# Encoder trunk in fp32r: scores of three neighbourhood groups as 128-row products of stacked keys and queries

## The chip, the cores and the metric

One core of one Trainium2 chip runs the whole kernel in one launch. The metric is the device time of one execution in microseconds (us), the median over the timed runs. The engines are named as the profile names them: PE is TensorE's matmul, PEld its weight load, DVE VectorE, ACT ScalarE, POOL GpSimd, SP SyncE, which issues nearly all DMAs.

## The reference, cut to what matters

Two layers run on x, 1024 tokens by 1024 features, in fp32. Each layer takes h = RMSNorm(x), projects it to the queries, keys and values of two kinds of heads and to a gate, attends, multiplies by silu(gate), projects back and adds to x. A final RMSNorm follows.

```python
# differential heads: 4 heads, two 64-wide halves each
s = einsum('bqhcd,bkhcd->bhcqk', qi, k) * scale - slope * |i - j|
p = softmax(s); a = p[:, :, 0] - lam * p[:, :, 1]; o = a @ v
# neighbourhood heads: 8 heads of width 64, a grid of 16 rows x 64 columns
s = einsum('bnqhd,brnkhd->bhnqrk', qr, kb) * scale   # 8 grid rows, 16 columns around each query
s = where(col_valid, s + bias, -inf); p = softmax(s); o = p @ v
```

The change concerns only the products of queries and keys of the neighbourhood heads.

## The kernel before, in words

**Arithmetic.** Every fp32 operand of a product is split in two fp32r parts, hi (a rounded copy that ACT writes) and lo (the rest, a subtraction on DVE or POOL). A product of two such operands is three matmuls: hi times hi, hi times lo and lo times hi; lo times lo is left out. `three` (L1134) does this for the projections.

**Groups and steps.** A layer has eight groups (`Group`, L192): four of one differential head each, then four of two neighbourhood heads each. A group has eight query tiles of 128 tokens, one for each step t. While a group attends, PE also runs the projections in pieces (`group_piece`, 24 matmuls of 512 columns each, for half of the tokens): pieces 0 and 1 of a group are its own gate, 2 to 7 the values, keys and queries of the next group, two pieces each. Piece t runs in step t, piece 0 of the next group in step 8, split in three parts that stand between the attention work. The last neighbourhood group projects no next one (`project=False`); output rows fill its steps. `from_second` (L543) and `steps` (L530) walk the steps in the same order on each engine; the order within a step is written out by hand in PE's `step` (L1319), DVE's `step` (L1734), ACT's `attend` (L1005) and POOL's `attend` (L774).

**Scores.** `score` (L1158) computes the scores of both heads of a tile (m = 0 and 1). Head m has its 64 features in partitions 64m to 64m+63 of `q_hi`, `q_lo`, `k_hi` and `k_lo`, so each matmul contracts over 64 rows of the array; the inner loop goes over m, so two products stand next to each other that use different halves of the rows. A neighbourhood tile in positions 0 to 3 (image tiles 0, 1, 6, 7; "edge") has 512 keys, one in positions 4 to 7 (tiles 2 to 5; "inner") has 576, of which 64 are computed by separate matmuls, ahead for m = 0 and behind for m = 1 (`tail`, L1179). An edge tile takes 6 matmuls, an inner tile 12. PE runs `score` of tile t+1 in the middle of step t, between the two transposes of tile t-1's probabilities, and `score` of the next group's tile 0 in step 7, of its tile 1 in step 8.

**The other engines in a neighbourhood step.** DVE adds the bias and takes the row maxima (`shifted`, L1632); ACT takes the exponentials (`exponentials`, L960); POOL divides by the sums (`weigh_rows`, L740); PE transposes the result (`turn_p`, L1216, L1231); ACT writes the hi part (`p_part`, L951, L940), DVE the lo part (L1659); every second step PE multiplies by the values (`weigh_pair`, L1268, L1282 and L1283), ACT and DVE take the product out (`output_half`, L975; `output_pair`, L1701).

**Queries and keys of the next group.** DVE writes key pieces 4 and 5 to `k_next` and query pieces 6 and 7, one after the other, to `q_next` (`piece_part`, L1603). ACT copies them to `k_hi` (L936, in step 6, after PE has read the keys for the last time) and `q_hi` (L930, steps 6 and 8). DVE makes `k_lo` (L1630) at the start of step 7, POOL makes `q_lo` (`q_lo_part`, L709). POOL also makes the lo parts of the weights (`w_lo_part`, L693, 128 columns by 8), in step 6 those of the next group's gate, as soon as ACT has made the hi part (L898). `load_chunk` (L599) on SP loads the next weights when that lo part is done.

## Time and profile before

| | us |
|---|---|
| median of 3 runs | 1426.14 (1425.80 to 1426.84) |
| the profiled execution | 1425.85 |
| its span, first to last instruction | 1424.0 |
| PE busy, of the span | 1410.6 (99%) |
| POOL, DVE, ACT busy | 651.9, 879.0, 692.9 |
| mean granted TensorE clock | 0.998 of full |

The profiled execution took 1425.85 us as a run, 1.85 us more than the span of its records. A busy PE is not the same as a PE at its peak: matmuls are pipelined, and a record lasts from the first column in to the last result out, so neighbouring records overlap. The distance from start to start is what a matmul costs the stream.

### The profile page before, as it was taken

To read this page: it belongs to the slowest core of one execution; us is meant where nothing else is said; L and a number is where in the kernel's file an instruction comes from. 1 tells how busy PE (TensorE), PEld (TensorE's weight loads), DVE (VectorE), ACT (ScalarE), POOL (GpSimd) and SP (SyncE) were. 2 spreads that over 40 slices of the span, in tenths; PEclk is the share of its full clock that TensorE was granted. 3 is DMA by queue.
4 is the path that set the end of the run, shared out by engine and by line. 5 is a ranking of instruction groups with operands and counts; after the bars stand their busy time and mean duration, and the time that the engine had idled before them with its cause. 6 is when DMAs were issued, how large, how long until landed. Compare 5 with 4: busy or idle time off the path is not lost.

```text
span 1424.0 us, 23782 instructions
## 1 busy us (share of the span) xinstructions
PE 1410.6 (99%) x8148; PEld 1155.3 (81%) x8148; DVE 879.0 (62%) x1815; ACT 692.9 (49%) x1376; POOL 651.9 (46%) x490
## 2 busy tenths in 40 slices
PE   9999999999999999999999999999999999999997
PEld 7788887888888888788887887888888888887887
DVE  7767677767655565653337776767766555556434
ACT  6445555455444444652525555546454444457331
POOL 3223222234576667543643231323247666667243
PEclk9999999999999999999999999999999999999999
DMA  5710101121021112301210100100212121213113
GB/s 185 155 30 23 52 22 37 37 63 38 24 70 34 57 39 56 148 30 45 74 45 31 38 23 29 44 30 22 66 36 64 38 63 37 63 38 126 46 59 118
DMA packets 41850, 79.57 MB, mean 56 GB/s; under 512 B 19120, under 2 KB 21424, under 8 KB 41776
## 3 DMA queue, kind: packets, MB, share of 16 engines
q1 hardware_dynamic: 41632, 78.60, 17.6%
q8 instruction: 44, 0.72, 0.2%
q14 instruction: 30, 0.25, 0.1%
q10 hardware_dynamic: 144, 0.01, 0.0%
HBM read 66.57 MB, written 15.96 MB: 58 GB/s over the span
## 4 chain that ended last, share of the span: by engine, by line
PE 96%; DVE 1%; ACT 1%; issue 1%; DMA 1%; SPq 0%; POOLq 0%; POOL 0%; DVEq 0%; ACTq 0%
PE proj L1136 19%; PE proj L1138 19%; PE proj L1137 18%; PE scores L1172 12%; PE turn L1231 6%; PE mix L1282 3%; PE mix L1283 3%; PE scores L1231 2%; PE mix L1249 2%; PE mix L1248 2%; PE mix L1247 2%; PE scores L1136 1%; PE scores L1137 1%; PE scores L1138 1%; DMA xt<-x_t 1%
## 5 line engine op out<-in xcount | busy, mean ns | idle before, releaser
L1136 PE MATMUL proj<-h_hi,w_hi 128*128 128x512 f32 (+1 forms) x1184 | 487.3, 412 | 1.2 <-DVE h_lo L1534 1.1
L1138 PE MATMUL proj<-h_hi,w_lo 128*128 128x512 f32 (+1 forms) x1184 | 461.5, 390 | 0.0
L1137 PE MATMUL proj<-h_lo,w_hi 128*128 128x512 f32 (+1 forms) x1184 | 458.5, 387 | 0.0
L696 POOL TENSOR_TENSOR w_lo<-w_raw,w_hi 128x1024 fp32r<-128x1024 f32 x62 | 152.7, 2463 | 308.8 <-ACT w_hi L898 308.8
L1659 DVE TENSOR_TENSOR pt_lo<-turn,pt_hi 128x512 fp32r<-128x512 f32 (+1 forms) x208 | 139.1, 669 | 204.8 <-ACT pt_hi L940 203.5
L1138 PEld LDWEIGHTS proj<-h_hi,w_lo 128*128 128x128 f32 x1184 | 222.4, 188 | 49.2
L1136 PEld LDWEIGHTS proj<-h_hi,w_hi 128*128 128x128 f32 x1184 | 223.2, 188 | 41.8 <-issue 5.5
L1137 PEld LDWEIGHTS proj<-h_lo,w_hi 128*128 128x128 f32 x1184 | 224.0, 189 | 34.2
L940 ACT ACTIVATE pt_hi<-turn 128x512 fp32r<-128x512 f32 (+1 forms) x208 | 120.4, 579 | 202.4 <-PE turn L1231 201.1
L747 POOL TENSOR_SCALAR prob<-prob,rrec 128x512 f32<-128x512 f32 (+1 forms) x96 | 156.9, 1647 | 113.2 <-DVE rrec L1684 112.8
L1651 DVE CUSTOM_DVE_ANT_0 prob<-scores,inner 128x1024 f32<-128x1024 f32 (+1 forms) x192 | 203.5, 1060 | 3.6 <-PE scores L1172 3.2
L965 ACT ACTIVATE prob<-prob,nm,escale_now 128x1024 f32<-128x1024 f32 x128 | 158.7, 1239 | 57.5 <-DVE nm L1655 57.1
L1231 PE MATMUL turn<-ident,prob 128*128 128x128 f32 x768 | 118.6, 277 | 0.0
L965 ACT ACTIVATE prob<-prob,nm 128x576 f32<-128x576 f32 (+1 forms) x128 | 95.5, 747 | 46.3 <-DVE nm L1655 45.6
L1231 PEld LDWEIGHTS turn<-ident,prob 128*128 128x128 f32 x768 | 88.7, 140 | 31.2 <-issue 21.2
L1172 PE MATMUL scores<-k_hi,q_hi 64*128 64x512 f32 (+1 forms) x448 | 105.2, 428 | 0.0
L1659 DVE TENSOR_TENSOR pt_lo<-scores,pt_hi 128x512 fp32r<-128x512 f32 (+1 forms) x80 | 50.8, 636 | 82.7 <-ACT pt_hi L940 82.0
L940 ACT ACTIVATE pt_hi<-scores 128x512 fp32r<-128x512 f32 (+1 forms) x80 | 44.4, 554 | 105.2 <-PE scores L1231 104.3
L1172 PE MATMUL scores<-k_lo,q_hi 64*128 64x512 f32 (+1 forms) x448 | 94.9, 375 | 0.0
L1172 PE MATMUL scores<-k_hi,q_lo 64*128 64x512 f32 (+1 forms) x448 | 94.6, 374 | 0.0
L713 POOL TENSOR_TENSOR q_lo<-q_next,q_hi 128x512 fp32r<-128x512 f32 x32 | 44.3, 1383 | 97.2 <-ACT q_hi L930 97.2
L1691 DVE SCALAR_TENSOR_TENSOR prob<-prob,cmix 128x1024 f32<-128x1024 f32 x64 | 83.9, 1311 | 2.3
(191 smaller groups left out, 2328.2 us busy)
## 6 DMA issues: line engine op xcount, KB each, us to landing
w_raw<-chunks SPq DMA_DIRECT2D x80, 512.0 KB, 3.5
mixed_dram<-gate SPq DMA_DIRECT2D x28, 256.0 KB, 2.4
edge<-bias_dram SPq DMA_DIRECT2D x32, 224.0 KB, 4.9
h_lo<-mixed_dram SPq DMA_DIRECT2D x14, 512.0 KB, 6.6
xt<-x_t SPq DMA_DIRECT2D x8, 512.0 KB, 8.6
bias_dram<-bias_rows SPq DMA_DIRECT2D x16, 240.0 KB, 6.1
out_t<-xt SPq DMA_DIRECT2D x8, 256.0 KB, 2.1
out_t<-xt SPq DMA_DIRECT2D x16, 128.0 KB, 1.8
```

The source lines that it names most:

```text
L696: pool.tensor_tensor(w_lo[:, b], w_raw[:], f32(w_hi[:, b]), ALU.subtract).then_inc(w_lo_done, 1)
L747: pool.tensor_scalar(part, part, rrec[:, t % 4, m:m + 1], None, ALU.mult).then_inc(prob_scaled, 1)
L940: act.activation(dst, src, ACT.Copy).then_inc(turn_hi, 1)
L965: act.activation(s, s, ACT.Exp, bias=nm[:, b, m:m + 1], scale=scale, accum_out=rsum[:, b, m:m + 1]).then_inc(exp_done, 1)
L1136: pe.matmul(dst, a_hi, b_hi, start=start, stop=False)
L1137: pe.matmul(dst, a_hi, b_lo, start=False, stop=False)
L1138: return pe.matmul(dst, a_lo, b_hi, start=False, stop=stop)
L1172: return pe.matmul(out, (q_hi, q_lo, q_hi)[p][own, tile], (k_hi, k_hi, k_lo)[p][own, cols], start=p == 0, stop=p == 2)
L1231: last = pe.transpose(dst[:, k * P:(k + 1) * P], prob_of(g.na, t, m, first + k * P, first + (k + 1) * P), ident[:])
L1651: dve.tensor_tensor_reduce(prob_of(g.na, t, m, 0, w), all_scores[:, at:at + w], bias, 1.0, -3e38, ALU.add, ALU.max, mx[:, b, m:m + 1]).the ...
L1659: dve.tensor_tensor(dst, src, f32(hi), ALU.subtract).then_inc(turn_freed, 1)
L1691: dve.scalar_tensor_tensor(prob[:, b, :], prob[:, 2, :], cmix[:, b:b + 1], prob[:, b, :], ALU.mult, ALU.add).then_inc(comb_done, 1)
```

## The change

The groups concerned are neighbourhood groups 0, 1 and 2 of each layer; group 3 and the differential groups keep their products.

- `k_hi` and `k_lo` become two stacks for these groups, one for each head: stack m holds head m's hi keys in its own 64 partitions and head m's lo keys in the other 64 (two ACT copies and two DVE subtractions of 64 x 1024, `k_stack_part`). DVE does its part at the end of step 6 instead of the start of step 7.
- `q_hi` and `q_lo` become rings of four tiles by two heads. For each tile ACT writes head m's hi queries to both halves of the partitions (four copies of 64 x 128, `stack_hi_part`), DVE the lo queries to the head's own half (two subtractions of 64 x 128, `stack_lo_part`); the other half of the lo queries holds zeros, written once for a layer (`clear_stacks`, two memsets of 64 x 512).
- With 128 rows a matmul with the hi stack is hi times hi plus hi times lo, one with the lo stack is lo times hi. So an edge tile takes 4 matmuls of 512 columns, an inner tile 8, of 384 and 192 columns, since the 576 are cut at a bank's edge and placed anew in PSUM (`window`, `SPANS`).
- ACT does a tile's copies three steps ahead of its front (the next group's tile 0 in step 6, tile 1 in step 7, tiles 2 and 3 in step 8); DVE's follow, for most tiles one step later. The raw queries stay in `q_next` and in the second half of `k_next`. POOL's `q_lo_part` and ACT's copies to `q_hi` go for these groups.
- PE waits for each tile's lo queries (`stack_lo`), POOL waits in step 6 for the low keys before it makes the lo part of the next gate's weights.

The counters' declarations and the numbering of `q_ready` (`queries`, `next_queries`) are left out below.

```diff
@@ -98,6 +98,10 @@
     WIDTH = [576 if INNER[t] else 512 for t in range(NT)]
+    SPANS = [[[(0, 384), (384, 576)], [(0, 192), (192, 576)]] if INNER[t] else [[(0, HALF)]] * 2 for t in range(NT)]
+    STACKS = 4
     STEP0 = {na: min(t for t in range(NT) if TILE[na][t] >= NT // 2) for na in TILE}
@@ -195,6 +199,9 @@
             self.g = i + (DA_G if na else 0)
+            self.stacks = na and project
+            last_of = NA_G - 2 if na else DA_G - 1
+            self.to_stacks = project and na != (isinstance(i, int) and i == last_of)
         def step(self, t):
@@ -344,6 +358,28 @@
             return prob[:, 2 if m else t % 2, first:end]
+        k_stack = (k_hi, k_lo)
+        def stack(buf, t, m):
+            at = (2 * (t % STACKS) + m) * P
+            return buf[:, at:at + P]
+        def raw_queries(t):
+            tile = TILE[True][t]
+            part = k_next[:, HALF:] if tile >= NT // 2 else q_next[:]
+            return part[:, tile % 4 * P:(tile % 4 + 1) * P]
+        def stacked_hi(g, behind, t):
+            if t >= NT - 2:
+                return [(behind, i) for i in ([0], [1], [2, 3])[t - (NT - 2)]] if g.to_stacks else []
+            return [(g, t + 3)] if g.stacks and t < NT - 3 else []
+        def own(m):
+            return slice(m * HD, (m + 1) * HD)
         def pair_cols(na, t):
@@ -373,8 +409,10 @@
             return all_scores[:, 3 * HALF:] if g.na and g.order().get(key, 0) % 2 else turn[:]
-        def window(t, m):
+        def window(g, t, m):
+            if g.stacks and INNER[t]:
+                return (P, HALF + 320)[m]
             return m * (3 * HALF - WIDTH[t])
@@ -775,6 +816,8 @@
                         weigh_rows(front, ft)
+                    if g.to_stacks and t == NT - 2:
+                        pool.wait_ge(k_lo_done, g.group() + 2)
                     if front and front.projects(ft) and ft % 2 == 0:
@@ -791,7 +834,7 @@
                         normalise(g, (t - 3) // 2)
-                    if front and front.projects(ft) and ft // 2 == Q_:
+                    if front and front.projects(ft) and ft // 2 == Q_ and not front.to_stacks:
                         q_lo_part(front, ft)
@@ -923,7 +966,9 @@
                     act.activation(gate_tanh[:], gate[:, cols], ACT.Tanh).then_inc(piece_half, 1)
-                if kind == Q_:
+                if kind == Q_ and g.to_stacks:
+                    act.nop().then_inc(piece_half, 1)
+                elif kind == Q_:
                     act.wait_ge(piece_freed, g.freed(t) + 1)
@@ -933,7 +978,22 @@
                 act.wait_ge(piece_freed, g.freed(2 * K_ + 1) + 1)
-                act.activation(k_hi[:], k_next[:], ACT.Copy).then_inc(k_hi_done, 1)
+                if g.to_stacks:
+                    for m in range(2):
+                        last = act.activation(k_stack[m][own(m)], k_next[own(m)], ACT.Copy)
+                    last.then_inc(k_hi_done, 1)
+                else:
+                    act.activation(k_hi[:], k_next[:], ACT.Copy).then_inc(k_hi_done, 1)
+            def stack_hi_part(g, t):
+                act.wait_ge(qk_done, g.step(t) - 3)
+                act.wait_ge(piece_freed, g.piece(0) - (TILE[True][t] < NT // 2))
+                for m in range(2):
+                    for to in range(2):
+                        last = act.activation(stack(q_hi, t, m)[own(to)], raw_queries(t)[own(m)], ACT.Copy)
+                last.then_inc(stack_hi, 1)
             def turn_part(g, key, dst, src):
@@ -1047,6 +1107,8 @@
                             piece_part(g, t)
+                    for to, i in stacked_hi(g, behind, t):
+                        stack_hi_part(to, i)
                     for i in rows[1]:
@@ -1159,21 +1221,34 @@
                     pe.wait_ge(k_lo_done, g.group() + 1)
-                    pe.wait_ge(q_ready, 2 * g.group() + 1)
+                if g.stacks:
+                    if t == 0:
+                        pe.wait_ge(stack_zero, 2 * (g.l + 1))
+                    pe.wait_ge(stack_lo, g.scaled(t) + 1)
+                    first = KEY0[t] * W
+                    for m in range(2):
+                        for a, b in SPANS[t][m]:
+                            out = all_scores[:, window(g, t, m) + a:window(g, t, m) + b]
+                            keys = k_stack[m][:, first + a:first + b]
+                            pe.matmul(out, stack(q_hi, t, m), keys, start=True, stop=False)
+                            last = pe.matmul(out, stack(q_lo, t, m), keys, start=False, stop=True)
+                    last.then_inc(qk_done, 1)
+                    return
+                if t == 0:
+                    pe.wait_ge(q_ready, g.queries(0) + 1)
                 if t == STEP0[g.na]:
-                    pe.wait_ge(q_ready, 2 * g.group() + 2)
+                    pe.wait_ge(q_ready, g.queries(1) + 1)
                 tile = slice(TILE[g.na][t] * P, (TILE[g.na][t] + 1) * P)
...
                 def product(m, p, at, a, b):
-                    own = slice(m * HD, (m + 1) * HD)
                     out, cols = all_scores[:, at + a:at + b], slice(first + a, first + b)
-                    return pe.matmul(out, (q_hi, q_lo, q_hi)[p][own, tile], (k_hi, k_hi, k_lo)[p][own, cols],
+                    return pe.matmul(out, (q_hi, q_lo, q_hi)[p][own(m), tile], (k_hi, k_hi, k_lo)[p][own(m), cols],
                                      start=p == 0, stop=p == 2)
-                at = [window(t, m) if g.na else m * S for m in range(2)]
+                at = [window(g, t, m) if g.na else m * S for m in range(2)]
                 spans = [[(0, HALF)], [(WIDTH[t] - HALF, WIDTH[t])]] if g.na else [[(0, HALF), (HALF, S)]] * 2
@@ -1620,10 +1695,37 @@
                     reached(dve, piece_done, n + 1)
-                    if not (isinstance(g, First) and g.l + t % 2 == 0):
-                        dve.wait_ge(q_ready, g.l * 2 * GROUPS + 2 * (g.g + 1) + t % 2)
-                    dve.scalar_tensor_tensor(q_next[:], ps, qscale[:, bass.ds(g.g + 1, 1)], rbc[:, cols],
+                    dst = k_next[:, HALF:] if g.to_stacks and t % 2 else q_next[:]
+                    if not (g.to_stacks and t % 2) and not (g.na and t % 2 == 0) and \
+                            not (isinstance(g, First) and g.l + t % 2 == 0):
+                        dve.wait_ge(q_ready, g.next_queries(t % 2))
+                    dve.scalar_tensor_tensor(dst, ps, qscale[:, bass.ds(g.g + 1, 1)], rbc[:, cols],
                                              ALU.mult, ALU.mult).then_inc(piece_freed, 1)
+            def stack_lo_part(g, t):
+                dve.wait_ge(stack_hi, g.scaled(t) + 1)
+                for m in range(2):
+                    rows = own(m)
+                    last = dve.tensor_tensor(stack(q_lo, t, m)[rows], raw_queries(t)[rows], f32(stack(q_hi, t, m)[rows]),
+                                             ALU.subtract)
+                last.then_inc(stack_lo, 1)
+            def clear_stacks(g):
+                dve.wait_ge(qk_done, g.l * (GROUPS * NT) + DA_G * NT)
+                for m in range(2):
+                    part = q_lo[own(1 - m), :].rearrange("p (s m c) -> p s m c", m=2, c=P)[:, :, m]
+                    dve.memset(part.bitcast(F32), 0.0).then_inc(stack_zero, 1)
+            def k_stack_part(n):
+                dve.wait_ge(k_hi_done, n + 1)
+                for m in range(2):
+                    last = dve.tensor_tensor(k_stack[m][own(1 - m)], k_next[own(m)], f32(k_stack[m][own(m)]),
+                                             ALU.subtract)
+                last.then_inc(k_lo_done, 1)
             def k_lo_part(n):
@@ -1745,8 +1847,14 @@
                     shift_scores(front, ft)
-                if g.project and t == NT - 1:
+                if g.project and not g.to_stacks and t == NT - 1:
                     k_lo_part(g.group() + 1)
+                if g.to_stacks and not g.na and t == NT - 1:
+                    clear_stacks(g)
+                if g.to_stacks and t == NT:
+                    stack_lo_part(behind, 1)
+                if g.stacks and t <= NT - 3:
+                    stack_lo_part(g, t + 2)
                 for c in range(3 if g.na and INNER[t - 1] else 2):
@@ -1769,6 +1877,11 @@
                 add_pieces(2)
+                if g.to_stacks and t == NT - 2:
+                    k_stack_part(g.group() + 1)
+                    stack_lo_part(behind, 0)
+                if g.to_stacks and t == NT:
+                    stack_lo_part(behind, 2)
                 if g.na and t % 2 == 0:
```

## Rows read from the trace of the kernel before

**Rows 1.** The page: part 1, busy time by engine; part 2, PE's busy tenths in 40 slices.
```profile
PE 1410.6 (99%) x8148; PEld 1155.3 (81%) x8148; DVE 879.0 (62%) x1815; ACT 692.9 (49%) x1376; POOL 651.9 (46%) x490
...
PE   9999999999999999999999999999999999999997
```
**Rows 2.** Waits of PE and PEld: us in total, times, longest us.
```profile
PE mix L1282 <- DVE pt_lo L1659: 1.3, 6, 0.3
...
PEld scores L1172 <- issue: 40.3, 120, 0.4
```
**Rows 3.** Timeline of PE (start us, us, engine, line), scores of an edge tile.
```profile
499.22 0.40 PE L1137 MATMUL proj<-h_lo,w_hi 128*128 128x512 f32 x1
499.45 0.40 PE L1138 MATMUL proj<-h_hi,w_lo 128*128 128x512 f32 x1
499.78 0.50 PE L1172 MATMUL scores<-k_hi,q_hi 64*128 64x512 f32 x2
500.12 0.39 PE L1172 MATMUL scores<-k_hi,q_lo 64*128 64x512 f32 x2
500.35 0.40 PE L1172 MATMUL scores<-k_lo,q_hi 64*128 64x512 f32 x2
500.68 0.66 PE L1231 MATMUL scores<-ident,prob 128*128 128x128 f32 x4
```
**Rows 4.** Timeline of PE: transposes alone, then the scores of an inner tile.
```profile
541.49 0.60 PE L1231 MATMUL turn<-ident,prob 128*128 128x128 f32 x4
541.84 0.47 PE L1136 MATMUL proj<-h_hi,w_hi 128*128 128x512 f32 x1
...
543.08 0.40 PE L1138 MATMUL proj<-h_hi,w_lo 128*128 128x512 f32 x1
543.40 0.51 PE L1172 MATMUL scores<-k_hi,q_hi 64*128 64x64 f32 x2
...
544.63 0.66 PE L1231 MATMUL scores<-ident,prob 128*128 128x128 f32 x4
545.04 0.47 PE L1136 MATMUL proj<-h_hi,w_hi 128*128 128x512 f32 x1
```
**Rows 5.** Timeline of PE: products of 256 and of 128 columns, with 128-row weights.
```profile
510.94 0.28 PE L1283 MATMUL mix<-pt_lo,v_hl 128*128 128x256 f32 x1
511.06 0.22 PE L1282 MATMUL mix<-pt_hi,v_hl 128*128 128x128 f32 x1
...
511.23 0.27 PE L1282 MATMUL mix<-pt_hi,v_hl 128*128 128x128 f32 x1
511.34 0.27 PE L1283 MATMUL mix<-pt_lo,v_hl 128*128 128x128 f32 x1
```
**Rows 6.** One neighbourhood group in windows: us, then busy us and instructions of each engine.
```profile
427.70:499.78 72.08, 72.08 (x425) 59.34 (x424) 40.75 (x103) 34.16 (x72) 48.64 (x30) 1.00 0.16 50
```
**Rows 7.** Instructions by source line: duration ns min/median/max, first and last start.
```profile
L1630 DVE TENSOR_TENSOR k_lo<-k_next,k_hi x16: 1218/1271/2577, 43.7 to 1270.0; 128x1024 fp32r<-128x1024 f32 x16
...
L1712 DVE TENSOR_TENSOR gate<-u,gate x32: 424/426/1811, 389.5 to 1356.8; 128x256 f32<-128x256 f32 x32
...
L1730 DVE MEMSET inner<- x8: 165/165/165, 383.1 to 1292.0; 64x128 f32 x8
```
**Rows 8.** Groups by line and form: busy us, mean ns, idle before.
```profile
L980 ACT ACTIVATE u<-mix 64x256 f32<-64x256 f32 x32 | 12.2, 382 | 60.0 <-PE mix L1283 59.7
```
**Rows 9.** Timelines of DVE and PE, hand-over from differential to neighbourhood heads, layer 0.
```profile
351.22 1.47 DVE L1630 TENSOR_TENSOR k_lo<-k_next,k_hi 128x1024 fp32r<-128x1024 f32 x1
354.87 0.69 DVE L1659 TENSOR_TENSOR pt_lo<-turn,pt_hi 128x512 fp32r<-128x512 f32 x1 [2.18 <-ACT pt_hi L940]
...
355.44 0.50 PE L1172 MATMUL scores<-k_hi,q_hi 64*128 64x512 f32 x2
```
**Rows 10.** Timelines of DVE and PE, step 2 of layer 0's first neighbourhood group.
```profile
383.70 0.69 DVE L1659 TENSOR_TENSOR pt_lo<-turn,pt_hi 128x512 fp32r<-128x512 f32 x1 [0.22 <-DVE inner L1731]
384.38 0.67 DVE L1659 TENSOR_TENSOR pt_lo<-scores,pt_hi 128x512 fp32r<-128x512 f32 x1
...
385.59 0.28 PE L1282 MATMUL mix<-pt_hi,v_hl 128*128 128x256 f32 x1
```

More of the change, by code:

```diff
@@ L219, in group, with queries, next_queries @@
             return self.l * GROUPS + self.g
+        def queries(self, hf):
+            return 2 * (self.l * (DA_G + 1) + (DA_G if self.na else self.i)) + hf
+        def next_queries(self, hf):
+            return 2 * (self.l * (DA_G + 1) + (DA_G if self.na else self.i + 1)) + hf
         def order(self):
@@ L261, in __init__ @@
             self.l, self.na, self.i, self.g, self.project = l, False, -1, -1, True
+            self.stacks = self.to_stacks = False
         def freed(self, t):
@@ L462, in hybrid_encoder @@
         tail_done = sem("tail_done")
+        stack_hi = sem("stack_hi")
+        stack_lo = sem("stack_lo")
+        stack_zero = sem("stack_zero")
         qk_done = sem("qk_done")
@@ L1192, in score @@
                 if wide:
-                    pe.wait_ge(tail_done, (g.l * NA_G + g.i) * sum(INNER) + sum(INNER[:t]) + 1)
+                    pe.wait_ge(tail_done, g.l * sum(INNER) + sum(INNER[:t]) + 1)
                     last = tail(1, 0, WIDTH[t] - HALF)
@@ L1649, in shifted @@
                     bias = edge[:, m, first:first + w]
-                at = window(t, m) if g.na else m * S
+                at = window(g, t, m) if g.na else m * S
                 dve.tensor_tensor_reduce(prob_of(g.na, t, m, 0, w), all_scores[:, at:at + w], bias, 1.0, -3e38, ALU.add, ALU.max,
```

## The prediction

> **What bounds the kernel now.** I read the page first: PE is busy for 99% of the span and for nine tenths or more in every slice but the last, its weight loads for 81%, and no other engine is over 62% [rows 1]. Then the waits of PE: inside the layers the longest group of waits is 1.3 us in six pieces, all in the last neighbourhood group, which the change leaves alone [rows 2]. So PE never starves here; the end moves only if its stream gets shorter, or if another engine becomes late. Since records overlap, I price everything on PE by the distance from start to start in its timeline. A projection matmul of 512 columns takes 499.45 - 499.22 = 0.23 us [rows 3].
>
> Now the block that is changed. In an edge tile the last projection starts at 499.45 and the next transposes at 500.68, 1.23 us later; less the projection's own 0.23 that is 1.00 us for the scores [rows 3]. The six matmuls stand as three rows "x2": the two heads' 64-row products start together and share a slot. Three slots of 0.23 would be 0.69; the other 0.31 are gaps: 0.33 before the first pair instead of 0.23, 0.34 to the second, 0.33 from the last to the transposes [rows 3]. PEld says what the gaps are: it stands still before score weights for 40.3 us in 120 places, 0.34 us each, with nothing to wait for that the profile shows [rows 2]. Transposes feel it too: after a score block they need 545.04 - 544.63 = 0.41 us to the next projection, without one 541.84 - 541.49 = 0.35, so 0.06 more belongs to the scores [rows 4]. An inner tile costs 544.63 - 543.08 - 0.23 = 1.32 and the same 0.06 [rows 4]. The gaps stand where the stream goes from 128-row to 64-row matmuls and back; between projections and transposes, both with 128 rows, there is none on the way in.
>
> **The change, part by part.** *Edge tiles.* Four matmuls of 512 columns at 0.23 are 0.92, with no change of row mode. Gain: 1.00 + 0.06 - 0.92 = 0.14 us. There are 24: four in each of three groups, two layers. 24 x 0.14 = 3.4 us.
>
> *Inner tiles.* Eight matmuls, four of 384 columns and four of 192. For 384, between 0.12 at 256 columns [rows 5] and 0.23 at 512 [rows 3], I take the columns' share, 0.173. For 192 the trace has two bounds: the column share of 0.23 is 0.086; but 128-column products with 128-row weights don't go below 511.34 - 511.23 = 0.11, and 256 columns take 0.12 [rows 5], so a floor that does not depend on the columns lies near 0.115. I take 0.115, since both neighbours stand there. Block: 4 x 0.173 + 4 x 0.115 = 1.15. Gain: 1.32 + 0.06 - 1.15 = 0.23 us, 24 x 0.23 = 5.5 us; at 0.086 it would be 2.8 us more.
>
> PE's stream gets 8.9 us shorter if nobody is late.
>
> *ACT.* Goes: two query copies and one key copy of 128 x 1024. New: two key copies of the same width (one more 1024-column copy) and 4 x 8 copies of 64 x 128 a group. The nearest row has twice the columns, 0.38 us [rows 8]; from 0.2 to 0.38 each makes 6 to 12 us a group, against 72.08 - 34.16 = 37.9 us idle [rows 6]. Behind each set of four in ACT's queue stand the exponentials or the taking out of the value product; both wait for DVE or PE in most steps by now, so I cost it at nothing. Step 8, with two sets (1.6 to 3 us), is the fullest; without that cover the value transposes' copies and the first scores would slip.
>
> *DVE.* New: the key subtraction twice over (each 1.22 undisturbed [rows 7], since 64 partitions take no less time than 128), 16 small subtractions of 0.2 to 0.4 a group, and the zeros once a layer. Some 6 us a group against 31.3 idle [rows 6]. Here place counts. At the hand-over from differential heads, k_lo starts at 351.22 and PE begins the first neighbourhood scores at 355.44 [rows 9]. In that stretch DVE now does 2 x 1.22 to 353.66, two small subtractions to 354.3 (or 354.8, since POOL's weight part has just been released and DVE's SBUF operations stretch beside POOL: 424 to 1811 ns for the same gate product, 1218 to 2577 for k_lo [rows 7]), then two memsets of 64 x 512. A memset of a quarter of the columns takes 0.165 [rows 7]; so between 0.17 and 0.66 each, and I take 0.5, near the column share. That gives 355.3 to 355.8 for PE's 355.44, and the p_part that began at 354.87 [rows 9] begins up to 0.9 later. I put 0.2 us of PE wait (0 to 1) on each of two such hand-overs, 0.1 (0 to 1) on each of the four between neighbourhood groups, which have no memsets but the output pair in the same place. In step 2 of a layer's first neighbourhood group the bias copy is already late: p_part starts at 383.70, its second half ends at 384.38 + 0.67 = 385.05, and PE needs it at 385.59 [rows 10]. Two small subtractions now stand ahead, 0.4 to 1.1 us against a margin of 0.54, so 0.1 (0 to 0.6) in each of two places. Sum: 0.4 + 0.4 + 0.2 = 1.0 us, from 0 to 7.2.
>
> *POOL.* Goes: two q_lo of 512 columns for each group. The new wait holds the weight part of step 6 until DVE's low keys are done, at about 353.7 in the hand-over just told. Queued behind it are POOL's division by the sums (or the norm factors) of step 7, which waits for DVE's reciprocal in step 7 anyway, and SP's next weight load, which ACT wants only late in step 8. Who waits for the weight part itself is PE's piece 0 in step 8; ahead of it, after 355.44, stand the scores, the transposes and nine matmuls of piece 7, 0.9 + 0.4 + 9 x 0.23 = 3.4 us. POOL has all the time from 353.7 to 358.8 for one part. Cost: nothing; without that cover, the excess over 5.1 us would show six times.
>
> *Sum.* 8.9 - 1.0 = 7.9 us off the profiled execution's 1425.85 (its span 1424.0 and 1.85 around it) is 1417.95. The median lies 0.29 higher, so 1418.2.
>
> **The rivals.** *Slower: the gaps stay.* If the 0.31 + 0.06 us around a score block belong to the change of operands and banks and not to the row mode, a block keeps 0.37. Then an edge tile costs 0.92 + 0.37 = 1.29 against 1.06, an inner one 1.15 + 0.37 = 1.52 against 1.38: 24 x 0.23 + 24 x 0.14 = 8.9 us more, with 1.0 of waits 1436.0. The point from which it decides is a gap of some 0.18 us left per block. For it: by slots alone the change is a loss, 4 for 3. Against it: transposes read other operands into other banks and follow a projection after 0.23. The Trainium skill, TensorEngine Tiling (Array Packing), speaks on both sides: section Theoretical Speedup gives contractions of at most 64 up to twofold throughput, which this change gives up, and section Key Properties says that a change of the tiling mode drains the engine. By the first alone the kernel gets slower; the trace shows both, pairs in one slot and the gaps at their two ends.
>
> *Hand-overs late.* DVE's small operations run at their stretched prices or ACT's copies come late, and the waits come to 5 us instead of 1.0: 1422.2. For it: DVE's spread beside POOL [rows 7]. Against it: DVE and ACT are idle over 40% of a group [rows 6].
>
> *No change in effect.* A wait of 0.18 us a step in all 48 steps, from DVE's lo queries behind ACT's copies, would eat the gain: 1426. Against it: the copies are made a step ahead.
>
> *192 columns at their column share.* 2.8 us more: 1415.4.
>
> **How the numbers follow.** Forecast 64%; late hand-overs 14%; 192 columns cheap 9%; no change 5%; gaps stay 8%. The range reaches to both neighbours on the faster side and takes in the bounds of the waits up to 5 us: 1414.8 to 1422.6. A change under 0.2% (2.9 us) can't be told from none. Faster: 64 + 14 + 9 = 87%; same 5%; slower 8%.
>
> **What would show it.** Right: score matmuls of 128 rows, 0.92 us a block in edge tiles, near 1.15 in inner ones, 0.35 us for the transposes behind; PEld's idle time before scores falls by some 48 places of the 120; PE's busy share stays at 99%, and DVE appears in PE's waits with about 1 us, at step 7. Wrong: gaps over 0.1 us at the ends of the 128-row blocks; PE waits on lo queries in most steps; 192-column products at 0.09 or over 0.12; POOL as releaser of piece 0.

## The result: 1431.1 us against 1426.2

| | before | after |
|---|---|---|
| median of 6 runs, us | 1426.17 (1425.80 to 1426.84) | 1431.09 (1429.97 to 1431.89) |
| profiled execution, its span | 1425.85, 1424.0 | 1431.87, 1430.0 |
| mean granted clock | 0.998 | 0.995 |
| predicted | | 1418.2 (1414.8 to 1422.6) |

The ratio is 1.0033, with a 95% interval from 1.0023 to 1.0044: slower by a third of a per cent, where I had forecast a gain of half a per cent. The six runs stand in two clusters, three near 1430.2 us and three near 1431.9; the median lies between them, and the profiled execution belongs to the upper one.

The page after, part 1, answers to [rows 1]:

```profile
PE 1408.2 (98%) x8004; PEld 1167.5 (82%) x8004; DVE 926.5 (65%) x1921; ACT 750.0 (52%) x1562; POOL 637.5 (45%) x478
```

PE has 144 matmuls fewer and is busy 2.4 us less, though the span is 6.0 us longer. So the loss is not in its stream of work; it must lie in waits.

First the part that went as planned. The timeline of PE after, an edge tile and then an inner tile, answers to [rows 3, 4]:

```profile
379.56 0.39 PE L1233 MATMUL scores<-k_hi,q_hi 128*128 128x512 f32 x1
...
380.24 0.40 PE L1234 MATMUL scores<-k_lo,q_lo 128*128 128x512 f32 x1
380.47 0.60 PE L1306 MATMUL scores<-ident,prob 128*128 128x128 f32 x4
380.83 0.48 PE L1198 MATMUL proj<-h_hi,w_hi 128*128 128x512 f32 x1
...
419.53 0.34 PE L1233 MATMUL scores<-k_hi,q_hi 128*128 128x384 f32 x1
419.70 0.35 PE L1234 MATMUL scores<-k_hi,q_lo 128*128 128x384 f32 x1
419.89 0.25 PE L1233 MATMUL scores<-k_hi,q_hi 128*128 128x192 f32 x1
419.98 0.27 PE L1234 MATMUL scores<-k_hi,q_lo 128*128 128x192 f32 x1
420.09 0.27 PE L1233 MATMUL scores<-k_lo,q_hi 128*128 128x192 f32 x1
...
420.31 0.36 PE L1233 MATMUL scores<-k_lo,q_hi 128*128 128x384 f32 x1
420.51 0.34 PE L1234 MATMUL scores<-k_lo,q_lo 128*128 128x384 f32 x1
420.68 0.60 PE L1306 MATMUL turn<-ident,prob 128*128 128x128 f32 x4
```

Edge block: 380.47 - 379.56 = 0.91 us, the transposes behind it 0.36. Inner block: 420.68 - 419.53 = 1.15 us, the predicted sum, but partly by luck: the four 384-column products took 0.73 us (0.17 to 0.20 each) where I had 0.69, and the four of 192 columns 0.42 (0.09 to 0.11 each) where I had 0.46. The first edge product starts 0.23 behind the projection at 379.33, and the others stand 0.22 to 0.23 apart. There is no gap at either end.

Then the waits. Waits of PE and PEld after (us in total, times, longest) answer to [rows 2]:

```profile
PE scores L1233 <- DVE q_lo L1720: 4.9, 2, 2.4
PE turn L1302 <- DVE pt_lo L1761: 3.0, 6, 0.6
PE scores L1233 <- DVE q_lo L1711: 1.9, 4, 0.5
...
PE mix L1357 <- DVE pt_lo L1761: 1.2, 6, 0.3
...
PEld scores L1247 <- issue: 24.1, 72, 0.4
```

PEld's idle places before scores went from 120 to 72, the 48 that were expected. But three groups of PE's waits are new or larger: twice 2.4 us for the zeros in q_lo (L1720), four times about 0.5 for the low queries (L1711), and four more waits for pt_lo in the transposes. These ten new waits lie at the six hand-overs, in step 7 of the group before: I call the two from differential to neighbourhood heads the long ones, the four between neighbourhood groups the short ones. The value products (mix) wait for pt_lo no more than before (1.2 in 6), so step 2 is not hurt.

What happened there is seen in the timelines of DVE and POOL after, at the first hand-over from differential to neighbourhood heads:

```profile
352.16 1.22 DVE L1726 TENSOR_TENSOR k_lo<-k_next,k_lo 64x1024 fp32r<-64x1024 f32 x1
353.41 2.68 DVE L1711 TENSOR_TENSOR q_lo<-q_next,q_hi 64x128 fp32r<-64x128 f32 x2
356.15 0.48 DVE L1720 MEMSET q_lo<- 64x512 f32 x1
356.80 0.48 DVE L1720 MEMSET q_lo<- 64x512 f32 x1 [0.16 <-issue]
...
353.46 2.48 POOL L737 TENSOR_TENSOR w_lo<-w_raw,w_hi 128x1024 fp32r<-128x1024 f32 x1 [11.95 <-DVE k_lo L1726]
```

Two subtractions of 64 x 128 take 2.68 us. Undisturbed they take 0.58, as the source line shows:

```profile
L1711 DVE TENSOR_TENSOR q_lo<-q_next,q_hi x48: 270/289/2394, 353.4 to 1240.8; 64x128 fp32r<-64x128 f32 x48
```

One of the pair took its 0.29, the other 2.39, nearly the length of POOL's weight part (2.48). POOL's subtraction was released by DVE's own k_lo and began 0.05 us after DVE had begun the pair: the new wait starts the one operation that gets in DVE's way at the moment when DVE is most in a hurry. All six hand-overs show a pair of 2.68 or 2.69. PE's timeline has the consequences, first at that hand-over, then at one between two neighbourhood groups:

```profile
357.54 0.77 PE L1233 MATMUL scores<-k_hi,q_hi 128*128 128x512 f32 x1 [2.44 <-DVE q_lo L1720]
358.10 0.63 PE L1234 MATMUL scores<-k_hi,q_lo 128*128 128x512 f32 x1
358.53 0.63 PE L1233 MATMUL scores<-k_lo,q_hi 128*128 128x512 f32 x1
...
430.75 0.50 PE L1233 MATMUL scores<-k_hi,q_hi 128*128 128x512 f32 x1 [0.47 <-DVE q_lo L1711]
...
432.82 0.44 PE L1302 MATMUL turn<-ident,prob 128*128 128x128 f32 x2 [0.44 <-DVE pt_lo L1761]
```

After the long wait the products stand 0.43 us apart instead of 0.23. The windows say why (us; busy us and instructions of PE, PEld, DVE, ACT, POOL; granted clock; DMA share; GB/s):

```profile
353.00:357.54 4.54, 2.10 (x14) 1.53 (x12) 4.25 (x6) 3.25 (x9) 3.79 (x4) 0.99 0.14 19
357.54:361.00 3.46, 3.46 (x11) 2.83 (x12) 2.04 (x4) 0.47 (x1) 0.00 (x0) 0.52 0.61 205
361.00:364.00 3.00, 3.00 (x15) 2.43 (x14) 2.77 (x8) 1.34 (x6) 0.00 (x0) 1.00 0.00 0
```

For 3.46 us PE is granted 0.52 of its clock, near the lower of its two levels, 1.2 GHz, and then 2.4 GHz again. Before it fell, PE had worked at full clock and then stood still for 2.4 us. That costs up to 3.46 x 0.48 = 1.7 us more. At the second such hand-over the same happened: PE stood still for 2.43 us, and from 1060.41 to 1063.87 the clock was 0.53. The DMAs that ran in this window (share 0.61) do not explain it: in experiment 3 their share is 0.70 just behind the standstill, at a clock of 1.00.

### The profile page after: what moved, and what is told of

It is laid out like the page before. It is cut to its first block, busy times and chain, and to the rows that moved or that the text cites. A ratio compares the mean times of both kernels' runs of the same rounds, so it can differ in the third digit from the quotient of the medians.

```text
span 1430.0 us, 23876 instructions
## 1 busy us (share of the span) xinstructions
PE 1408.2 (98%) x8004; PEld 1167.5 (82%) x8004; DVE 926.5 (65%) x1921; ACT 750.0 (52%) x1562; POOL 637.5 (45%) x478
## 4 chain that ended last, share of the span: by engine, by line
PE 91%; DVE 5%; issue 2%; ACT 1%; DMA 1%; SPq 0%; DVEq 0%; POOLq 0%; POOL 0%; ACTq 0%
PE proj L1198 18%; PE proj L1200 18%; PE proj L1199 18%; PE scores L1247 8%; PE turn L1306 6%; PE mix L1357 2%; PE mix L1358 2%; PE mix L1324 2%; PE mix L1323 2%; PE mix L1322 2%; PE scores L1306 2%; PE scores L1233 2%; PE scores L1234 2%; DVE q_lo L1711 1%; DVE prob L1753 1%
## 5 line engine op out<-in xcount | busy, mean ns | idle before, releaser
L737 POOL TENSOR_TENSOR w_lo<-w_raw,w_hi 128x1024 fp32r<-128x1024 f32 x62 | 153.0, 2468 | 331.7 <-ACT w_hi L941 289.6
L1357 PE MATMUL mix<-pt_hi,v_hl 128*128 128x256 f32 (+1 forms) x320 | 77.0, 281 | 1.2 <-DVE pt_lo L1761 1.2
L1358 PE MATMUL mix<-pt_lo,v_hl 128*128 128x256 f32 (+1 forms) x320 | 75.9, 281 | 0.0
L748 POOL TENSOR_TENSOR w_lo<-w_raw,w_hi 128x1024 fp32r<-128x1024 f32 x15 | 37.2, 2480 | 82.3 <-ACT w_hi L1141 82.3
L1324 PE MATMUL mix<-pt_hi,v_hl 128*128 128x256 f32 x256 | 72.4, 283 | 0.0
```

The source lines that it names most:

```text
L737: pool.tensor_tensor(w_lo[:, b], w_raw[:], f32(w_hi[:, b]), ALU.subtract).then_inc(w_lo_done, 1)
L1357: pe.matmul(out, weights, pt_hi[:, m, at], start=n == 0, stop=False)
```

## The experiments

All but the fourth are the changed kernel with the edit shown. The kernel before, on the chips of these runs, had medians of 1426.10 (first four) and 1426.21 us.

**1. POOL does not wait.** The change has two parts that can be taken apart, and the wait is the suspect.

```diff
-                    if g.to_stacks and t == NT - 2:
-                        pool.wait_ge(k_lo_done, g.group() + 2)
```

> The changed kernel without POOL's wait for the low keys. Theory A (collision): in the changed kernel POOL's weight part of step 6 is released at the end of the key subtractions and runs beside DVE's first small query subtraction, which is then held for nearly the whole of it (2394 ns at most against 289 ns median). Without the wait POOL does that part some 4 us earlier, beside the key subtraction at worst; PE's waits at the six hand-overs (4.9 + 1.9 + 1.76 us) mostly go, and with them the half clock behind the two long ones: about 9 to 11 us less than the changed kernel, near 1419 to 1422 us. If the early weight part catches a key subtraction instead, a part of the waits stays. Theory B (queue length): DVE's queue at the hand-over is too long by itself, two key subtractions, two small ones and two memsets, and POOL's part matters little: within 2 us of the changed kernel's 1431.1, PE waits of about 2 us at both long hand-overs.

Measured: 1427.29 us (1426.72 to 1428.09), ratio 1.0008 (0.9998 to 1.0017). Without the wait the kernel takes 3.8 us less, but it is no better than before, and not the 1419 to 1422 that I expected. What happened is the case that the expectation reserved: POOL's part meets a key subtraction, and a part of the waits stays. Its timelines of DVE and POOL, and the largest group of PE's waits:

```profile
423.15 3.33 DVE L1724 TENSOR_TENSOR k_hi<-k_next,k_hi 64x1024 fp32r<-64x1024 f32 x1
...
422.99 2.40 POOL L737 TENSOR_TENSOR w_lo<-w_raw,w_hi 128x1024 fp32r<-128x1024 f32 x1 [1.75 <-ACT w_hi L939]
```

```profile
PE scores L1231 <- DVE q_lo L1718: 3.4, 2, 1.7
```

POOL's part now starts earlier and holds the key subtraction instead: it began at 423.15, POOL's ended at 422.99 + 2.40 = 425.39, and 1.09 us later DVE's was done, against 1.22 for the whole of it undisturbed. It made next to no progress beside POOL. At the long hand-overs the same subtraction took 2.56 us (350.83). So the wait was there to avoid a hold, and only moved it one operation on. The waits at the short hand-overs stay as they were; at the long ones PE waits 1.7 us instead of 2.4, and the half clock is gone (window of this kernel, same columns):

```profile
356.69:360.00 3.31, 3.31 (x17) 2.73 (x18) 3.02 (x6) 1.58 (x6) 0.00 (x0) 1.00 0.00 0
```

**2. POOL waits past the pair.** If POOL's part must start later still, one semaphore on from k_lo is the pair itself.

```diff
-                        pool.wait_ge(k_lo_done, g.group() + 2)
+                        pool.wait_ge(stack_lo, behind.scaled(0) + 1)
```

> The changed kernel with POOL's wait of step 6 put on tile 0's low queries instead of the low keys, so 0.6 us later when nothing disturbs. Theory A: no DVE operation of the pair meets the weight part; small subtractions all under 0.7 us; the zeros are written by 355 us instead of 357.3, PE waits under 0.3 us at the long hand-overs and the clock stays whole: 1418 to 1420 us. Theory B: POOL's place does not matter: 1430 to 1432.

Measured: 1421.99 us (1421.57 to 1422.67), ratio 0.9972 (0.9961 to 0.9984). One wait that ends 0.6 us later turns a loss of 4.9 us into a gain of 4.1. The pair takes 0.58 again (353.62), the memsets beside POOL's part take 0.48 as always, and PE waits for the zeros 0.7 us in all, with no half clock. It missed the expected 1418 to 1420 mainly because of a later operation in DVE's queue (DVE and POOL, then PE's waits):

```profile
425.18 0.42 DVE L1807 TENSOR_TENSOR u<-mix,u 64x256 f32<-64x256 f32 x1
425.61 0.43 DVE L1808 TENSOR_TENSOR u<-mix,u 64x256 f32<-64x256 f32 x1
426.08 1.93 DVE L1814 TENSOR_TENSOR gate<-u,gate 128x256 f32<-128x256 f32 x1
...
425.32 2.40 POOL L737 TENSOR_TENSOR w_lo<-w_raw,w_hi 128x1024 fp32r<-128x1024 f32 x1 [5.13 <-DVE q_lo L1711]
```

```profile
PE turn L1302 <- DVE pt_lo L1761: 3.6, 6, 0.6
```

The three rows tell what kind of operation is held. The two u operations read the mix from PSUM and one operand from SBUF: 0.42 and 0.43, though they run beside POOL. The gate product has both operands in SBUF: 1.93, where 0.42 is its price [rows 7]; it ends 0.29 us behind POOL's 427.72. It stands between the pair and pt_lo, so the third transposes wait.

**3. No zeros.** The rival held the two memsets and the clearing guilty.

```diff
-                    if t == 0:
-                        pe.wait_ge(stack_zero, 2 * (g.l + 1))
...
-                if g.to_stacks and not g.na and t == NT - 1:
-                    clear_stacks(g)
```

> The changed kernel without the two memsets that write the zeros and without PE's wait for them (POOL's wait for the low keys stays). It leaves out the zeros in the other head's half of the low queries, so its scores contain stale data. It prices the memsets and the clock. Theory A: the small subtractions still end at about 356.1, PE waits about 1.0 to 1.3 us at the two long hand-overs instead of 2.44, and if so short a wait does not halve the clock, another 1.5 us each is saved: 5 to 6 us less than the changed kernel, 1425 to 1426. Theory B's reading, in which the memsets are the cause: waits go altogether at the two long hand-overs, 1423.

Measured: 1426.29 us (1425.32 to 1427.16), ratio 0.9999 (0.9989 to 1.0009). PE's waits:

```profile
PE scores L1231 <- DVE q_lo L1709: 4.2, 6, 1.1
```

Without memsets PE still waits 1.1 us in the long hand-overs, for the held pair, and the four short ones are as they were. Between the medians it wins 4.8 us over the changed kernel, between the spans 1430.0 - 1424.7 = 5.3: that is about the 2 x 1.3 us of shorter wait and the half clock at both places, which is not there after a wait of 1.1 (clock 1.00 from 356.60 to 360.00). The reading that memsets alone make the loss, 1423, falls. But the memsets do add 1.3 us to each long wait.

**4. The products alone.** The kernel before with nothing of the change but PE's new products. It measures the gain with no cost on DVE, ACT or POOL.

```diff
...
+                if g.na and g.project:
+                    for m in range(2):
+                        for a, b in SPANS[t][m]:
+                            out = all_scores[:, window(g, t, m) + a:window(g, t, m) + b]
+                            keys = (k_hi, k_lo)[m][:, first + a:first + b]
+                            pe.matmul(out, q_hi[:, tile], keys, start=True, stop=False)
+                            last = pe.matmul(out, q_lo[:, tile], keys, start=False, stop=True)
+                    last.then_inc(qk_done, 1)
+                    return
...
```

> The kernel before with only PE's part of the change: in the three groups the score products contract over all 128 rows of the operands as they lie (q_hi and q_lo with k_hi for head 0, with k_lo for head 1), at the new widths and places in PSUM; nothing changes on ACT, DVE and POOL. Its scores are mixtures of both heads, so its output is not the reference's. It gives PE's gain by itself: by the sum of the prediction 24 x 0.14 + 24 x 0.23 = 8.9 us less than the kernel before, 1417.3 (1416.5 to 1418.5). If the shorter stream only moves the waits elsewhere, less: 1420 to 1424.

Measured: 1418.08 us (1417.6 to 1419.21), ratio 0.9945 (0.9929 to 0.9962); span 1415.9. PEld's row is that of the changed kernel, to the digit:

```profile
PEld scores L1184 <- issue: 24.1, 72, 0.4
```

So the products are worth 8.0 us against my 8.9, and everything else in the change costs 13.0.

**5. POOL waits for what comes last.** In hand-overs between neighbourhood groups POOL's part waits for the output pair, whose last operation is the gate product that was held in 2; in the others for the query pair.

```diff
-                    if g.to_stacks and t == NT - 2:
-                        pool.wait_ge(k_lo_done, g.group() + 2)
+                    if g.to_stacks and t == NT - 2 and g.na:
+                        pool.wait_ge(pair_done, g.pairs(2) + 1)
+                    elif g.to_stacks and t == NT - 2:
+                        pool.wait_ge(stack_lo, behind.scaled(0) + 1)
```

> The changed kernel with POOL's wait of step 6 put on tile 0's low queries at the hand-over from differential heads, and at the other two hand-overs of a layer on the output pair's gate product, the last DVE operation there that reads both operands from SBUF. Theory A, sharpened (a DVE operation with two SBUF operands does not move while POOL's two-input subtraction runs, whatever its own length; operations from PSUM and memsets do): the gate product, 1.93 us beside POOL's part when POOL waited for the low queries, comes back to 0.43, and the four waits of 0.58 us at the third transposes go to near zero; about 2.3 us less than with the wait on the low queries (1422.0), so 1419.7. Theory B (DVE's queue is simply too long there): the waits of about 0.5 us stay, 1421.5 to 1422.5.

Measured: 1419.2 us (1418.48 to 1419.51), ratio 0.9952 (0.9938 to 0.9966). DVE, POOL, and PE's waits:

```profile
425.65 0.43 DVE L1816 TENSOR_TENSOR gate<-u,gate 128x256 f32<-128x256 f32 x1
...
426.24 2.40 POOL L737 TENSOR_TENSOR w_lo<-w_raw,w_hi 128x1024 fp32r<-128x1024 f32 x1 [6.50 <-DVE gate L1816]
```

```profile
PE turn L1304 <- DVE pt_lo L1763: 1.3, 2, 0.6
...
PE scores L1235 <- DVE q_lo L1722: 0.7, 2, 0.3
```

The four waits of the third transposes are gone; the two that stay were there before, outside the hand-overs. Of the engines only SP waits for POOL's part, to load the next weights, though the part now starts 3 us later than in experiment 1.

**6. The zeros on POOL.** As 5 (whose edit is not shown again), with the zeros written by POOL in step 6, once the scores that still read q_lo are done, and taken out of DVE's queue.

```diff
-                if g.to_stacks and not g.na and t == NT - 1:
-                    clear_stacks(g)
...
+                        pool.wait_ge(edge_masked, MASK_PARTS * (g.l * NA_G + 1))
+                        pool.wait_ge(qk_done, g.l * (GROUPS * NT) + DA_G * NT)
+                        for m in range(2):
+                            part = q_lo[(1 - m) * HD:(2 - m) * HD, :].rearrange("p (s m c) -> p s m c", m=2, c=P)[:, :, m]
+                            pool.memset(part.bitcast(F32), 0.0).then_inc(stack_zero, 1)
+                        pool.wait_ge(stack_zero, 2 * (g.l + 1))
...
```

> As the run before it, and the zeros are written by POOL, which is idle in step 6, instead of DVE in step 7. Takes 1.2 us out of DVE's queue before the first neighbourhood scores. Theory A: the last waits at the two long hand-overs (0.33 us each) go too, about 0.5 to 0.8 us less: 1419.0. If POOL's memset disturbs DVE's combination of the probabilities, the same or 1 us more.

Measured: 1417.61 us (1417.03 to 1417.98), ratio 0.9941 (0.9927 to 0.9955); span 1415.1.

```profile
345.34 1.09 POOL L826 MEMSET q_lo<- 64x512 f32 x2 [4.07 <-PE scores L1255]
```

```profile
PE turn L1310 <- DVE pt_lo L1769: 1.3, 2, 0.6
PE mix L1365 <- DVE pt_lo L1769: 1.3, 6, 0.3
```

That is 1.6 us less than 5, where 0.5 to 0.8 was expected; the rest was not taken apart. PE now waits for DVE nowhere that it did not wait before. This is the best version: 8.6 us under the kernel before and 13.5 under the changed one, and its time is that of the products alone.

**7. POOL's part in halves.** One question of mechanism was left: is DVE stretched by a shared rate, or held until POOL's instruction ends? The changed kernel, its wait kept, with POOL's part as two instructions of half the length.

```diff
-                        w_lo_part(front.chunk(ft) + 1, 1 - front.buffer(ft))
+                        if g.to_stacks and t == NT - 2:
+                            c, b = front.chunk(ft) + 1, 1 - front.buffer(ft)
+                            pool.wait_ge(w_hi_done, c + 1)
+                            for ks in (slice(0, NT // 2), slice(NT // 2, NT)):
+                                last = pool.tensor_tensor(w_lo[:, b, ks], w_raw[:, ks], f32(w_hi[:, b, ks]), ALU.subtract)
+                            last.then_inc(w_lo_done, 1)
+                        else:
+                            w_lo_part(front.chunk(ft) + 1, 1 - front.buffer(ft))
```

> The changed kernel, its wait for the low keys kept, with POOL's weight part of step 6 cut in two subtractions of 512 columns, about 1.25 us each. Theory A: DVE's first small subtraction is held for the first half only and gets in between the halves; then either the second small one is held for the second half (hold as before in sum, 1431) or both get in before it: PE's waits at the long hand-overs 1.2 to 1.4 us instead of 2.44 and no half clock, 1424 to 1426. A theory of slowed but moving DVE operations (C: bandwidth shared while both run) expects no difference, as the same columns pass in the same time: 1431.

Measured: 1422.31 us (1422.03 to 1422.85), ratio 0.9974 (0.9965 to 0.9984).

```profile
353.99 1.59 DVE L1718 TENSOR_TENSOR q_lo<-q_next,q_hi 64x128 fp32r<-64x128 f32 x2
...
354.04 2.68 POOL L826 TENSOR_TENSOR w_lo<-w_raw,w_hi 128x512 fp32r<-128x512 f32 x2 [11.95 <-DVE k_lo L1733]
...
L1718 DVE TENSOR_TENSOR q_lo<-q_next,q_hi x48: 273/289/1296, 354.0 to 1232.1; 64x128 fp32r<-64x128 f32 x48
```

With nearly the same POOL work (2.68 us instead of 2.48) DVE's held operation takes 1.30 us instead of 2.39: it waits for one half of that work, not for the whole. A shared rate would have left the pair at 2.68. DVE is held until the POOL instruction that is under way ends, and gets its turn before the next. The Trainium skill, SBUF — State Buffer, section SBUF: two separate sides, says that a DVE operation with two SBUF inputs and a GpSimd operation that reads SBUF exclude each other for the whole length of an instruction; by that rule DVE's operation waits for POOL's current instruction and no longer, and the trace agrees: 2.39 us beside one of 2.48, 1.30 beside halves of 1.34. One case that does not fit is told in the last section. The time is below the expected 1424 to 1426, which had counted the long hand-overs alone (PE waits 1.35 us there, at full clock): PE's four waits for the low queries at the short ones are gone too, and those of the third transposes are down from 3.0 us in all to 2.0.

## Why the prediction was wrong

**PE's stream: right.** The predicted gain was 3.4 + 5.5 = 8.9 us; products alone gave 8.0. From block to block in the trace an inner tile gained 0.21 us (predicted 0.23) and an edge tile 0.12 on average (0.14). The rival that the gaps stay (1436.0) is refuted by the timeline, though its side, slower, came true by another road. The 192-column products, 0.105 on average, lie nearer to my 0.115 than to 0.086.

**ACT at nothing: right.** A set of four copies took 1.27 us (350.99), within the bounds of 0.2 to 0.38 each, and PE waited for none of them.

**Memsets: right.** 0.48 each, where I took 0.5; the 0.16 between them I had left out.

**Step 2: harmless.** No wait came where I put 2 x 0.1.

**The failed step is the price of DVE's two small query subtractions, and with it POOL's wait at nothing.** I had them done "to 354.3 (or 354.8 ...)", 0.6 or 1.1 us for the pair; they were done at 353.41 + 2.68 = 356.09, though the key subtractions had begun 0.3 us earlier than I took (350.93). From the maxima of [rows 7] (424 against 1811, 1218 against 2577) I read that DVE's operations stretch beside POOL, and so scaled the price with the operation: double of a small one is still small. The rows showed something else: 2577 - 1271 and 1811 - 426 are 1.3 and 1.4 us for operations of 1.27 and 0.42, so the excess does not grow with the operation. A look at the one of 2577 ns in the trace of before would have told what it depends on (DVE and POOL):

```profile
736.55 2.58 DVE L1630 TENSOR_TENSOR k_lo<-k_next,k_hi 128x1024 fp32r<-128x1024 f32 x1 [1.34 <-ACT k_hi L936]
...
735.65 2.40 POOL L696 TENSOR_TENSOR w_lo<-w_raw,w_hi 128x1024 fp32r<-128x1024 f32 x1 [8.85 <-ACT w_hi L898]
```

POOL's ends at 738.05, DVE's 1.08 us later. The k_lo of [rows 9] says the same: POOL's part there ran to 351.60,

```profile
349.20 2.40 POOL L696 TENSOR_TENSOR w_lo<-w_raw,w_hi 128x1024 fp32r<-128x1024 f32 x1 [7.29 <-ACT w_hi L898]
```

and k_lo, begun at 351.22, ended at 352.69, again 1.09 later, with an excess of only 0.25. That the two maxima exceed by nearly the same amount is chance: both operations began 0.9 us after POOL's. The price of a hold is what is left of POOL's instruction, up to 2.4 us, whatever the size of DVE's; and the change put the beginning of POOL's 2.4 us just behind the beginning of DVE's pair (0.05 us at the long hand-overs, 0.13 at the short ones). For POOL's wait I had asked who waits for the held-up operation, and rightly answered nobody. I had not asked what the operation does to others at the new place where it starts.

**The sum as it came out.** Spans: 1430.0 after, 1415.9 with the products alone, 14.1 us apart. The distances between matching score blocks of these two kernels put it in two places. At each of the two long hand-overs the block comes 2.6 us late and the next 1.6 more, by the half clock: 4.2. At each of the four short ones the block comes 0.65 late and the next 0.78 more: 1.42. 2 x 4.2 + 4 x 1.42 = 14.1. I had put all waits together at 1.0. A standstill costs more than the wait that the profile lists, because that begins where the last record ends: the last projection ahead of the first long wait ends at 354.70 + 0.40, but the next product would have started at 354.70 + 0.23. So 2.44 is 2.61, 0.47 is 0.64 and 0.44 is 0.61; 0.1 more is the first product behind a wait, which takes 0.33 to the next instead of 0.23.

**The range and chances.** My rival for late hand-overs had the right place and sign, but 5 us as its size, from stretched prices; it was 14, of which 2 x 1.6 are the half clock, which I had not priced at all. At that size it makes the kernel slower, and for slower I had only the 8% of a rival that came out wrong.

That the hold is the cause is shown from three sides: POOL's start moved back or forth moves it to another operation or past all of them (1, 2, 5), halving the instruction halves it (7), and with no hold at the hand-overs and the zeros out of DVE's queue the gain of the products is all there (6). The length of DVE's queue has a small part of its own: with the hold gone and the zeros still there, PE waits 0.34 us at each long hand-over (2, 5). That the half clock comes with the long standstill is seen in two places of one profile, and it is missing in the experiments with shorter ones; what exactly sets it off was not tried.

## What to carry to other kernels

Where a semaphore lets a two-input GpSimd operation go, look at what VectorE starts in the same microsecond: a VectorE operation with two SBUF operands then costs what is left of GpSimd's instruction, however small it is. Make GpSimd wait for the last such operation on VectorE's critical stretch, not for one in its middle, or cut GpSimd's instruction in pieces. And when a source line's durations spread, set each long one beside GpSimd's timeline: if it ends a fixed time after GpSimd's instruction, wherever it began (1.08 and 1.09 us here for an excess of 1.3 and of 0.25), it is a hold and not a slowdown; price it by what is left of the holder's instruction.

## What was not expected of the hardware

- A standstill of PE of 2.44 us (2.43 at the second long hand-over) was followed by 3.46 us at a granted clock of 0.52 (0.53); standstills of 1.68, 1.35 and 1.13 us were followed by a clock of 1.00. The two clusters of runs after, 1.6 us apart and with mean clocks of 0.995 and 0.996, would suit one such stretch more or less; only one run has a profile, so this stays open.
- The hold is not the same beside every POOL operation. Beside POOL's subtraction VectorE's memsets and its operations with one operand in PSUM were not held at all (0.48, 0.43, experiment 2). And beside POOL's TENSOR_SCALAR, which reads one tile from SBUF, the same pair of small subtractions took 0.58 to 0.99. Two such pairs, in DVE's and POOL's timelines after:

```profile
443.38 0.93 DVE L1711 TENSOR_TENSOR q_lo<-k_next,q_hi 64x128 fp32r<-64x128 f32 x2 [0.62 <-ACT q_hi L995]
465.37 0.58 DVE L1711 TENSOR_TENSOR q_lo<-q_next,q_hi 64x128 fp32r<-64x128 f32 x2
...
441.65 3.11 POOL L788 TENSOR_SCALAR prob<-prob,rrec 128x512 f32<-128x512 f32 x2 [5.17 <-DVE rrec L1786]
464.56 1.49 POOL L777 TENSOR_SCALAR gate_tanh<-gate_tanh 128x512 f32<-128x512 f32 x1
```

Both pairs lie wholly inside POOL's operations (to 444.76 and to 466.05) and neither waited for their ends. The Trainium skill's rule as told in experiment 7, for any GpSimd operation that reads SBUF, would hold both; for these the trace does not bear it out, and why is open.
- The hold works the other way round too. In the kernel before, POOL's q_lo of the first long hand-over began at 352.05, while DVE's k_lo ran to 352.69, and took 1.79 us; its usual price is 1.28 (the one at 424.02).
- In two of the three groups of a layer, one edge tile's block took 451.27 - 450.24 = 1.03 us where the others behind a projection take 0.91 to 0.93, 0.1 of it between the first two products. PEld loads the first weights there at 450.23, with the product, where for the block of 379.56 it loads them at 379.34; the products alone (experiment 4) show the same 1.03, and why the load comes late is open.
